# Spreading one value a token over all partitions by a transpose in place of a product with the identity, in a float32 two-model forward pass

## What is computed

```python
def rms_norm(x, g):
    xf = x.astype(jnp.float32)
    y = xf * lax.rsqrt(jnp.mean(xf * xf, axis=-1, keepdims=True) + RMS_EPS)
    return (y * g.astype(jnp.float32)).astype(x.dtype)

def l2_normalize(z):
    return z * lax.rsqrt(jnp.sum(z * z, axis=-1, keepdims=True) + 1e-12)
```

## Time and profile before

| | |
|---|---|
| time, median of 3 runs | 3788.41 us (3786.18 to 3791.53) |
| the profiled execution's own time | 3791.04 us |
| its span, first to last instruction | 3789.0 us |
| PE (matmul) busy | 3601.8 us, 95% |
| PEld (weight load) busy | 3321.8 us, 88% |
| DVE / ACT / POOL busy | 2102.6 / 1508.5 / 1660.3 us |
| mean granted TensorE clock | 0.976 of full |

### The profile page before, as it was taken

One profiled execution on the slowest core, in us unless ns is written; L12 is line 12 of the kernel. 1 busy time (PEld: TensorE's weight loads), 2 busy tenths in 40 slices (PEclk: granted clock), 3 DMA queues, 4 the chain that ended last, 5 costly groups with the idle time before them and its releaser, 6 DMA issues. The chain is left out here.

```text
span 3789.0 us, 86299 instructions
## 1 busy us (share of the span) xinstructions
PE 3601.8 (95%) x37216; PEld 3321.8 (88%) x37216; DVE 2102.6 (55%) x4000; ACT 1508.5 (40%) x2721; POOL 1660.3 (44%) x1195
## 2 busy tenths in 40 slices
PE   7999999999997999999979999999979999999998
PEld 7999898999996888888868888888869999999998
DVE  5544424544426776677666677766656553534343
ACT  5344434344434432232223334333334453534343
POOL 5555555555544543333321111111115566666664
PEclk9999999999999999999989999999989999999999
DMA  6444454444344776778610000100016444444443
GB/s 236 174 177 182 189 189 164 170 178 181 151 170 158 264 268 255 251 257 292 214 40 17 24 28 28 28 20 15 3 51 240 178 178 183 183 181 189 178 185 128
DMA packets 116394, 587.28 MB, mean 155 GB/s; under 512 B 20912, under 2 KB 40368, under 8 KB 51376
## 3 DMA queue, kind: packets, MB, share of 16 engines
q1 hardware_dynamic: 116016, 581.76, 41.4%
HBM read 561.00 MB, written 20.71 MB: 154 GB/s over the span
## 5 line engine op out<-in xcount | busy, mean ns | idle before, releaser
L570 PE MATMUL bank<-act_L,part_L 128*128 128x256 f32 x7296 | 946.2, 288 | 12.7 <-POOL act_L L3220 7.1
L570 PEld LDWEIGHTS bank<-act_L,part_L 128*128 128x128 f32 x7296 | 900.8, 193 | 49.4 <-issue 31.0
L3179 POOL TENSOR_TENSOR part_L<-wring,part_L 128x512 fp32r<-128x512 f32 x304 | 533.7, 1757 | 458.2 <-ACT part_L L1412 450.0
L570 PE MATMUL bank<-act_P,part_P 128*128 128x512 f32 (+1 forms) x3488 | 715.9, 365 | 18.0 <-POOL part_P L3179 12.7
L3179 POOL TENSOR_TENSOR part_C<-wring,part_C 128x512 fp32r<-128x512 f32 x320 | 567.3, 1781 | 370.8 <-ACT part_C L1412 370.8
L570 PEld LDWEIGHTS bank<-act_P,part_P 128*128 128x128 f32 x3488 | 590.2, 188 | 137.1 <-DVE arena_P L2552 16.1
L570 PE MATMUL bank<-arena_B 64*64 64x64 f32 (+2 forms) x11200 | 447.0, 237 | 51.0 <-DVE arena_B L2709 24.8
L3179 POOL TENSOR_TENSOR part_P<-wring,part_P 128x512 fp32r<-128x512 f32 x184 | 306.0, 1668 | 428.2 <-ACT part_P L1412 428.2
L1412 ACT ACTIVATE part_C<-wring 128x1024 fp32r<-128x1024 f32 x320 | 337.8, 1057 | 357.7 <-PE bank L570 355.3
L2155 DVE TENSOR_TENSOR part_L<-wring,part_L 128x512 fp32r<-128x512 f32 x304 | 237.5, 783 | 425.5 <-ACT part_L L1412 425.3
L570 PE MATMUL bank<-act_Y,part_C 128*128 128x258 f32 (+1 forms) x3840 | 464.1, 283 | 9.5 <-POOL part_C L3179 9.5
(11 more groups left out here) (256 smaller groups left out, 3467.1 us busy)
## 6 DMA issues: line engine op xcount, KB each, us to landing
wring<-in_w SPq DMA_DIRECT2D x404, 1024.0 KB, 4.9
arena_P<-in_w SPq DMA_DIRECT2D x64, 1024.0 KB, 5.2
mring<-in_w SPq DMA_DIRECT2D x32, 1024.0 KB, 6.9
z_kept<-arena_P SPq DMA_DIRECT2D x34, 256.0 KB, 5.7
z_kept<-arena_P SPq DMA_DIRECT2D x58, 128.0 KB, 5.3
xT<-z_kept SPq DMA_DIRECT2D x26, 256.0 KB, 2.6
arena_C<-z_kept SPq DMA_DIRECT2D x32, 128.0 KB, 2.8
cst<-z_kept SPq DMA_DIRECT2D x24, 128.0 KB, 2.1
```

The source lines that it names most:

```text
L570: return e.matmul(out, lhsT, rhs, start=start, stop=stop)
L3179: e.tensor_tensor(wl[:, 4:8, :], wring[s % NS][:, 8 * j + 4:8 * j + 8, :], wh[:, 4:8, :].bitcast(F32), sub).then_inc(*mark("pool_lo", "lop ...
```

## The change

The operands of the spreads stay what they are, and so does their place in PE's order. Where a spread covers all 128 partitions at once it is issued through `tr` and no longer through `mm`: the instruction has the same stationary operand (the broadcast column), the same moving operand (the identity) and the same output, and is marked as a transpose. The spreads of recurrence A (`heads` 2, 64 partitions each) stay products. No wait, no semaphore, no other engine's instruction and no DMA is touched.

```diff
@@ spread_norm
                 for m in range(2):
-                    t = mm(b[:, 128 * m:128 * m + 128], sm[:, step * m:step * m + 1].broadcast_to([128, 128]), ident, True, True)
+                    t = tr(b[:, 128 * m:128 * m + 128], sm[:, step * m:step * m + 1].broadcast_to([128, 128]))
                 t.then_inc(*mark("pe_norm", "spread", tag))
@@ spread
                     for q in range(heads):
-                        t = mm(b[wd * q:wd * q + wd, 128 * m:128 * m + 128],
-                               sm[:, heads * m + q:heads * m + q + 1].broadcast_to([128, wd]), ident, True, True)
+                        o, row = b[wd * q:wd * q + wd, 128 * m:128 * m + 128], sm[:, heads * m + q:heads * m + q + 1].broadcast_to([128, wd])
+                        t = tr(o, row) if heads == 1 else mm(o, row, ident, True, True)
                 t.then_inc(*mark("pe_sums", "spread", tag))
@@ gla
                     for m in range(2):
-                        t = mm(b2[:, 256 + 128 * m:384 + 128 * m], small(3)[:, m:m + 1].broadcast_to([128, 128]), ident, True, True)
+                        t = tr(b2[:, 256 + 128 * m:384 + 128 * m], small(3)[:, m:m + 1].broadcast_to([128, 128]))
                     t.then_inc(*mark("pe_gla", "spread", ("gla", l, h)))
```

## The result

The changed kernel takes 3807.12 us (median of 4 runs, 3801.95 to 3808.06), the kernel before 3788.68 (4 runs, 3786.18 to 3791.53). The ratio is 1.0045, with a 95% interval of 1.0031 to 1.0059: **slower by about 17 us**, where 12.6 us less were forecast. The profiled execution of the changed kernel took 3806.94 us; its span is 3805.1.

A forecast was written before the change was run, and what follows sets the result against it. TensorE, with matmuls busy for 95% of the span, was taken as the bound; savings of 3.0 + 1.35 + 3.4 + 1.3 + 3.6 = 12.65 us off the median 3788.4 gave 3775.8 us, range for 8 in 10 3769 to 3784.

The forecast's parts named there:

- Count and price of the bursts: All changed spreads: 220 matmul records become 110; a two-block burst takes 0.13 us among projections, 0.19 us after a wait.
- Stages L and P: Spreads outside recurrence B's heads: 0.23 us saved per saturated call, 1.35 us over five after waits, 0.43 us per entrance norm.
- Spreads of q and k pass on their saving: Eight heads of recurrence B: DVE idles until each spread, so q saves 3.4 us and k 3.6 us in all.
- rival 1: Heads of recurrence B: they swallow the savings of q and k, giving 3782.8 us; chance 0.13.
- Spread of o at nothing: Seven spreads of o: the 0.22 us PE saves at each returns as waiting; without that cover, 1.5 us more saved.
- rival 2: Heads: one more half-clock stretch in each of eight gives back 7.6 us, 3783.4 us; chance 0.09 for the bad side.
- its sign of being wrong: Mean clock over the heads falling below 0.93, named as the sign of rival 2 or Rival 3.
- Rival 3: Heads of recurrence B: transposes let the clock fall, 24 stretches cost 22.8 us, giving 3798.6 us; chance 0.03.
- Rival 4: All changed spreads: a transpose costs a quarter of the product, saving 19 us, giving 3769.4 us; chance 0.04.

The follow-up runs named there:

- `outside`: The change, but with the spreads of q, k and o in recurrence B's heads kept as products; ratio 0.9986 to the kernel before, 3787.35 us.
- both filled kernels: The change, and the kernel before, each with idle products in PE's pauses in the heads; 3760.17 us and 3766.13 us, ratios 0.9914 and 0.9933 to the latter unfilled.
- `kq_once`: The change with only the transposes of o issued twice; ratio 1.0031 to the kernel before, 3807.20 us.
- `kick`: The change with the four transposes of k issued five times in head 3 only; ratio 1.0026 to the kernel before, 3804.22 us.
- `twice`: The change with every transpose of q, k and o issued twice in place; ratio 0.9975 to the kernel before, 3782.01 us.
- `bf2`: The change with the spreads of q, k and o as bfloat16 products, each issued twice; ratio 1.0029 to the kernel before, 3805.80 us.
- `q_once`: The change with the transposes of k and o issued twice, those of q once; ratio 0.9964 to the kernel before, 3779.02 us.
- `k_once`: The change with the transposes of q and o issued twice, those of k once; ratio 0.9983 to the kernel before, 3784.54 us.

## Why the prediction was wrong

- **Count and price of the bursts: right.** 110 records went; a pair costs 0.14 and 0.19 us, against forecasts of 0.13 and 0.19. Stages L and P gave 4.4 us by the entrance of recurrence A (forecast, without ("M",0): 2.8 + 1.35 + 0.43 = 4.5), and `outside` gave 5.3 us as a whole (1.9 to 9.1 by its interval; forecast 5.2).
- **Spreads of q and k pass on their saving: right in mechanism, and hidden.** At a clock of 0.99 in both filled kernels a head gains 0.78 us. The sum had 0.43 + 0.45 = 0.88, of which 0.21 was the price at half clock. So rival 1, that the heads swallow the saving, doesn't hold.
- **Spread of o at nothing: no run speaks against it.** Doubling it (`kq_once`) left the time where it was: ratio 1.0031 to the kernel before against 1.0045, intervals that overlap. But both stand in the slow pattern, in which a head's length hardly follows its work, so this is no clean test. In the filled kernels the heads gain 0.11 us more than q and k account for, which is all that is left there for o's 0.22.
- **The step that failed is the clock.** The sum has no term for it, and rival 2 sized it as "one more" half-clock stretch in each head, 0.95 us each and 7.6 us in all, with a chance of 0.09 for the bad side. What came was 13.7 us more of half clock in each head (143.0 - 60.7 = 82.3 over six, or four stretches of 3.4 us a head and not one), and it cost far more than the spreads saved: the mean clock over the heads went to 0.90, under the 0.93 that the prediction had named as its sign of being wrong. Its price was too low as well. The six heads lost 24.35 us and had gained 4.7 by the shorter spreads, so 29.05 us for 82.3 us of half clock, an estimate of 0.35 us a microsecond against 0.28.
- **Why it was sized so.** I treated the stretches as independent falls, one more or one less. The rows could have warned me that the clock sets the length of a head: in the kernel before, two heads of equal work took 113.89 and 111.31 us, at clocks of 0.93 and 0.97. That the length in turn acts on the clock no row of the kernel before shows; `kick`, `twice` and `bf2` show it. A loop of equal heads with such feedback can settle into a pattern that repeats, and this pattern, with its 24 us of half clock, counted once for each head that was in it.
- **Rival 3 had the sign, by the wrong mechanism.** It wanted transposes to let the clock fall. `twice` and `bf2` exclude this here: transposes doubled leave the clock at 0.96, products of the same length have 0.90. The Trainium skill, "TensorE: Matmul & The Clock Gate", section "Part 4: PE-mode transpose", states that a transpose doesn't count as PE activity as a product does. By that rule I expected `twice` slow and `bf2` fast; at these sites, bursts of some 0.2 to 0.9 us in heads of 112 us, the runs show the opposite. (A slip in the working changes nothing: 20.2 us at 0.95 each are reached from 22 stretches on, and not from 21.)
- **Rival 4, a quarter of the price:** no; four transposes take 0.43 us where four products took 0.90, so one costs half, 0.11 us.

What stays open is which amount exactly tips the heads, and by which relation of pauses and clock the pattern holds itself. `q_once` (k doubled) is clear of the slow pattern, `k_once` seems near its edge, both shortened are in it. That was not resolved further.

## What to carry to other kernels

Where TensorE pauses and its clock falls again and again, as here, the length of a loop is no sum of its parts: 0.9 us less work in each head made the head 4 us longer, and 1.75 us of delay made one 3.75 us shorter. So look at the granted clock by loop pass before pricing a small edit; if it varies between passes of equal work, first fill the pauses with idle products and then measure the edit. Here the filling took 0.7% off the kernel before, and filling and change together took 0.9% off it, more than any edit of the spreads, and in the windows of the heads it made the effect of the edit readable.

## What the hardware showed that was not expected

- The heads settled into one length (116.02 to 116.04 us in the profile of the change, 116.04 in `bf2`, 116.08 to 116.26 in `kick` after one head out of line), in kernels that differ in when the heads begin and in what the spreads consist of.
- A transpose of a float32 block and its stationary load cost 0.11 us at full clock (four in 0.43 us), half of the product with the identity (four in 0.90), also when the block is one column repeated.
- Products that nobody reads, 6 before each of the two waits for line 2709 and 8 more at three other places of a head, raised the mean clock in the heads from 0.90 to 0.99 and took 7.6 us off a head (696.00 - 650.67 = 45.3 over six).
